# Encoder trunk kernel: four tiles for turned probabilities in the neighbourhood attention, weight splits and a GpSimd multiplication at other places

## The reference, cut to what matters

```
layer 0: x = x + concat(dilated_attention, latent_attention) @ w_out
         x = x + swiglu(rms_norm(x, ln_ffn_e))
layer 1: q, k, v = split(rms_norm(x, ln_mix_o) @ na_w_qkv)        # 16 heads of 64
         sc  = q @ k.T * 64**-0.5 + mask + rpb                    # 256 x 256 a head
         x   = x + (softmax(sc) @ v for every head) @ na_w_out
         logits = rms_norm(x, ln_ffn_o) @ moe_router              # 8 experts, 2 per token
         x   = x + sum over e: gates[:, e] * swiglu_e(rms_norm(x, ln_ffn_o))
out = rms_norm(x, ln_final)
```

## Time and profile before

| what | value |
|---|---|
| median of 3 runs | 1460.08 us (1459.95 to 1460.48) |
| the profiled execution | 1466.72 us, of which the span of the profile is 1464.8 us |
| PE busy | 1430.1 us, 98% |
| DVE, ACT, POOL busy | 1132.6, 969.0, 122.0 us |
| weights read | 426.98 MB from HBM |
| attention heads of layer 1 on PE | about 390 to 452 us from the start of the span |
| output projection | 456.5 to 478.7 us |
| router, to the first expert matmul | 478.4 to 498.4 us |
| experts | 498.4 us to the end |

### The profile page before, as it was taken

The page is one execution under the profiler, slowest core; times in us unless marked ns, Lnnn a source line. Parts: engine busy times, 40 slices in busy tenths (PEclk is TensorE's granted clock), DMA queues, the critical chain, the costliest instruction groups (busy, mean ns, idle before and its releaser), DMA issues.

```text
span 1464.8 us, 20962 instructions
## 1 busy us (share of the span) xinstructions
PE 1430.1 (98%) x7705; PEld 1228.1 (84%) x7705; DVE 1132.6 (77%) x892; ACT 969.0 (66%) x885; POOL 122.0 (8%) x101
## 2 busy tenths in 40 slices
PE   8989999999989999999999999999999999999996
PEld 7878999999988788888888888888888888888885
DVE  4484555556663798988988888888898898888886
ACT  6384543436463577777777777777777777777774
POOL 4141000000000310020001001002002000000100
PEclk8999999999999999999999999999999999999999
DMA  9413755555513599999999999999999999999992
GB/s 337 151 58 102 210 197 173 197 175 173 173 58 111 180 378 378 367 356 394 394 361 394 386 344 393 396 367 376 393 372 364 394 386 354 394 380 363 392 395 109
DMA packets 205562, 434.91 MB, mean 297 GB/s; under 512 B 8160, under 2 KB 53344, under 8 KB 205520
## 3 DMA queue, kind: packets, MB, share of 16 engines
q1 hardware_dynamic: 198176, 418.01, 78.4%
q0 software_dynamic: 3904, 14.42, 3.2%
q10 hardware_dynamic: 3440, 1.91, 0.7%
HBM read 426.98 MB, written 7.34 MB: 297 GB/s over the span
## 4 chain that ended last, share of the span: by engine, by line
PE 92%; DVE 4%; ACT 2%; issue 1%; DMA 0%; DVEq 0%; ACTq 0%
PE banks L1428 29%; PE banks L1430 29%; PE banks L1429 29%; PE banks L1841 2%; PE banks L1650 1%; DVE w_lo L880 1%; PE banks L1638 1%; ACT arena L619 0%; PE banks L1805 0%; DVE arena L1077 0%; DVE small L1083 0%; PE banks L1576 0%; ACT w_hi L469 0%; PE banks L1443 0%; DVE arena L1065 0%
## 5 line engine op out<-in xcount | busy, mean ns | idle before, releaser
L880 DVE TENSOR_TENSOR w_lo<-raw,w_hi 128x2048 fp32r<-128x2048 f32 (+1 forms) x396 | 902.6, 2291 | 223.4 <-ACT w_hi L469 222.0
L469 ACT CAST w_hi<-raw 128x2048 fp32r<-128x2048 f32 (+1 forms) x396 | 756.3, 1910 | 227.2 <-PE banks L1430 219.8
L1428 PE MATMUL banks<-w_hi,t_hi 128*128 128x512 f32 (+2 forms) x1088 | 417.9, 384 | 3.7 <-DVE w_lo L880 1.6
L1430 PE MATMUL banks<-w_lo,t_hi 128*128 128x512 f32 (+2 forms) x1088 | 412.0, 379 | 0.0
L1429 PE MATMUL banks<-w_hi,t_lo 128*128 128x512 f32 (+2 forms) x1088 | 410.9, 378 | 0.0
L1428 PEld LDWEIGHTS banks<-w_hi,t_hi 128*128 128x128 f32 x1088 | 206.2, 190 | 40.9 <-DVE w_lo L880 1.8
L1430 PEld LDWEIGHTS banks<-w_lo,t_hi 128*128 128x128 f32 x1088 | 206.1, 189 | 38.8
L1429 PEld LDWEIGHTS banks<-w_hi,t_lo 128*128 128x128 f32 x1088 | 206.4, 190 | 36.2 <-issue 0.2
L1428 PE MATMUL banks<-w_hi,h_hi 128*128 128x512 f32 x536 | 209.5, 391 | 0.7 <-DVE w_lo L880 0.7
L1430 PE MATMUL banks<-w_lo,h_hi 128*128 128x512 f32 x536 | 208.9, 390 | 0.0
L1429 PE MATMUL banks<-w_hi,h_lo 128*128 128x512 f32 x536 | 208.8, 390 | 0.0
(11 more groups left out here) (269 smaller groups left out, 944.6 us busy)
## 6 DMA issues: line engine op xcount, KB each, us to landing
raw<-in_moe_w_gate SPq DMA_DIRECT2D x112, 1024.0 KB, 7.5
raw<-in_moe_w_up SPq DMA_DIRECT2D x112, 1024.0 KB, 7.8
raw<-in_moe_w_down SPq DMA_DIRECT2D x112, 1024.0 KB, 7.7
raw<-in_na_w_qkv SPq DMA_DIRECT2D x12, 1024.0 KB, 5.2
raw<-in_ffn_w_gate SPq DMA_DIRECT2D x11, 1024.0 KB, 5.5
raw<-in_ffn_w_up SPq DMA_DIRECT2D x11, 1024.0 KB, 5.3
raw<-in_ffn_w_down SPq DMA_DIRECT2D x11, 1024.0 KB, 5.0
raw<-in_w_in_e SPq DMA_DIRECT2D x6, 1024.0 KB, 18.5
```

What stands on the lines that cost most here:

```text
L469: act.copy(w_hi[:, u.part, 0:n], raw[:, u.raw, 0:n]).then_inc(hi_done, 1)
L880: dve.tensor_tensor(w_lo[:, u.part, 0:n], raw[:, u.raw, 0:n], w_hi[:, u.part, 0:n].bitcast(F32), ALU.subtract).then_inc(lo_done, 1)
L1428: pe.matmul(out, a_hi, b_hi, start=start, stop=False)
L1430: return pe.matmul(out, a_hi, b_lo, start=False, stop=stop)
```

## The change

Four things are changed, all in layer 1.

1. Turned probabilities of heads 16 to 31 go through four buffers in turn: the two of `prob_t` and columns 512 to 1023 of the two tiles of `xn`. `prob_out(n)` waits for the values of head n-4 in place of n-2. In the steady loop `prob_out(n - 4)` stands ahead of `softmax(n)`; at the start `softmax(19)` stands ahead of `prob_out(16)`.
2. The three `hi` of the output projection move to the early part of ACT's queue, around `qkv_out(10)` and `qkv_out(11)`, and the three `lo` of DVE to after `row_max` 19, 21 and 22. PE runs `value_unit(2)` ahead of `turn_probs(16)` and `na_scores(4)` ahead of `turn_probs(17)`.
3. The first `keep_busy` has five dummy matmuls in place of eight.
4. GpSimd's two multiplications move to after the transfers of `xres` to `sum_d`.

```diff
+        turned = [prob_t[:, i, :] for i in range(2)]
+        turned_c = turned + [xn[:, t, HALF:D] for t in range(T)]
...
             def prob_out(n):
                 act.wait_ge(pt_mm, n + 1)
-                if n >= 2:
+                if n >= 16:
+                    act.wait_ge(pv_mm, max(n - 3, 16))
+                elif n >= 2:
                     act.wait_ge(pv_mm, n - 1)
-                act.copy(prob_t[:, n % 2, :], banks[:, T_BANK[n % 2], :]).then_inc(pt_out, 1)
+                act.copy(turned_c[n % 4] if n >= 16 else turned[n % 2], banks[:, T_BANK[n % 2], :]).then_inc(pt_out, 1)
...
             softmax(18, "neighbourhood", 2)
+            softmax(19, "neighbourhood", 3)
+            hi(Unit(U_OUT1))
+            qkv_out(10)
+            hi(Unit(U_OUT1 + 1))
             prob_out(16)
-            softmax(19, "neighbourhood", 3)
-            qkv_out(10)
+            softmax(20, "neighbourhood", 4)
             prob_out(17)
-            softmax(20, "neighbourhood", 4)
             softmax(21, "neighbourhood", 5)
-            hi(Unit(U_OUT1))
             qkv_out(11)
+            hi(Unit(U_OUT1 + 2))
             for n in range(22, 16 + CH + 4):
+                prob_out(n - 4)
                 if n < 16 + CH:
                     softmax(n, "neighbourhood", n - 16)
-                prob_out(n - 4)
-                if n in (23, 27):
-                    hi(Unit(U_OUT1 + n // 4 - 4))
...
                 row_max(n, "neighbourhood", n - 16)
-                if n in (21, 25, 29):
-                    lo(Unit(U_OUT1 + n // 4 - 5))
+                if n in (19, 21, 22):
+                    lo(Unit(U_OUT1 + (19, 21, 22).index(n)))
...
             na_scores(3)
+            value_unit(2)
             turn_probs(16)
-            value_unit(2)
+            na_scores(4)
             turn_probs(17)
-            na_scores(4)
             na_scores(5)
...
-            keep_busy(7, 8)
+            keep_busy(7, 5)
             pe.wait_ge(route_v, 1)
...
-            pool.wait_ge(x_tile, X_TILES[4])
-            pool.wait_ge(gain_in[3], 16)
-            for t in range(T):
-                pool.tensor_tensor(xn[:, t, :], xres[:, t, :], gain_rows[1], ALU.mult).then_inc(xg_ready, 1)
...
                 if not sweep:
-                    pool.wait_ge(xg_ready, T)
+                    pool.wait_ge(gain_in[3], 16)
                     for t in range(T):
+                        pool.tensor_tensor(xn[:, t, :], xres[:, t, :], gain_rows[1], ALU.mult).then_inc(xg_ready, 1)
+                    for t in range(T):
+                        pool.wait_ge(xg_ready, t + 1)
                         pool.dma_start(rows_d[t * P:(t + 1) * P, :], xn[:, t, :]).then_inc(rows_out, 16)
```

More of the change, by code:

```diff
@@ L1649, in values @@
                     for k in range(2):
-                        last = pe.matmul(banks[:, 4 + t, c:c + HD],
-                                         prob_t[:, n % 2, (2 * k + t) * P:(2 * k + t + 1) * P], v(k),
+                        p_t = turned_c[n % 4] if n >= 16 else turned[n % 2]
+                        last = pe.matmul(banks[:, 4 + t, c:c + HD], p_t[:, (2 * k + t) * P:(2 * k + t + 1) * P], v(k),
                                          start=(k == 0), stop=(k == 1))
```

## The result

| | before | after |
|---|---|---|
| median of 13 runs each, same chip | 1461.59 us (1459.95 to 1472.41) | 1455.15 us (1452.26 to 1458.11) |
| ratio | | 0.9939, 95% interval 0.9924 to 0.9955 |
| the profiled execution | 1466.72 us, span 1464.8 | 1454.66 us, span 1452.6 |

By the ratio the kernel is 8.9 us faster (1460.08 x 0.0061), between 6.6 and 11.1; the forecast was 10.8. The means of the 13 runs differ by 8.8 us, the two medians of the table only by 6.4. Two things are to be seen at once. The runs of one kernel spread over 6 us and more, so the profiled difference of 12.2 us between the spans is not the effect. And the medians moved with the set of runs (before stands at 1461.6 here, at 1460.1 in its first three), so the absolute 1455.15 lies above the range of 1447.0 to 1453.5, while the ratio, put to 1460.08, gives 1451.2, inside it.

The account below looks back on a forecast made before the run. It took PE, busy 98% of the span, to bound the kernel. Heads 7.2, transposes 0.3 and router 3.3 made 10.8 us, from 1460.1 to 1449.3 us; 8 in 10 for 1447.0 to 1453.5, own gain range 7.5 to 12.9.

Parts of the forecast that it names:

- Heads, 7.2 us: Heads 16 to 31: last values end at 444.6 instead of 451.8 us, 7.2 us earlier; bounds 5.5 and 7.5.
- Copy 18: ACT's copy of head 18's turned probabilities: runs 417.1 to 417.6 us, with 1.1 us to spare.
- the walk: Step-by-step timing of PE, ACT and DVE through the heads in the new order, ending at 444.6 us.
- The split into 6.0 of waits and 1.2 of clock: Of the heads' 7.2 us, 6.0 are waits and 1.2 the clock staying up without PE's 2.02 us wait.
- Four tiles: Heads: with two tiles the copy would wait for values n-2 and hold up the softmax behind it; no size given.
- The transposes, 0.3 us: The 16 transposes behind the heads: 0 to 1.2 us better, by where the lower clock falls; 0.3 taken.
- Router, 3.3 us: Router: DVE's chain and PE's small products start 3.3 us earlier; bounds 2.0 and 4.2 by the clock.
- One of the signs: Prediction wrong if PE's granted clock is 0.5 in stretches other than the few between heads, projection and router.
- `lo` at GpSimd's new place: Beside GpSimd's moved multiplications, one `lo` of DVE waits some 0.8 us, which PE does not see.
- The blocked DVE: Rival: DVE's L1275 waits for GpSimd's products at their new place, 1.5 to 2.9 us lost, 1451.5 us; 10%.
- ACT as the late one: Rival: in the heads ACT's copy 18 misses 418.8, half of the 6 us of waits remain, 1453.5 us; 10%.
- The clock falling in the heads: Rival, slower: heads 16 to 31 at 1.2 GHz, 3.7 us a head, 23 us more, 1473 us; 3%.

Follow-up runs that it names:

- e1: The kernel before with only the heads changed (four tiles, copy ahead, early splits); ratio to before 0.9955, 6.6 us faster.
- e3: The kernel after with the first dummies set back from five to eight; ratio to before 0.9930.
- e5: The kernel after with the old two tiles and the old wait for values n-2; heads 54.27 us in the profile, no ratio.
- e8: The kernel after with GpSimd's multiplications back at the old place, five first dummies kept; router stage 27.43 us in the profile, no ratio.
- e12: As e11, with four more dummies ahead of the transposes before the output projection; ratio to before 0.9923.
- e6: The kernel after with the copy behind the softmax again in the steady loop; heads 65.08 us in the profile, no ratio.
- e7: The kernel after with the three high and three low splits at their old places; heads 60.33 us in the profile, no ratio.
- e2: The kernel before with only the router changed (multiplications behind the transfers, five first dummies); ratio to before 0.9985, 2.2 us faster.
- e11: As e10, with six dummies ahead of each of the first two projection units of layer 0; ratio to before 0.9918.
- e4: The kernel after with eight first dummies and one dummy ahead of each of the eight k steps of the router logits; ratio to before 0.9915.
- e10: The kernel after with eight first dummies and one dummy ahead of every second k step of the router logits; ratio to before 0.9938.

## Why the prediction was right, and where not

- *Heads, 7.2 us.* Right in size and in each step: 7.15 in the profile, 54.21 to 54.27 in every kernel that has both order and splits (e1, e3 to e5, e8 to e12), and 6.6 us (4.2 to 9.1) in the timed runs of e1. Copy 18, the wait of `values(24)` and the last values came within 0.2 us of the walk. The split into 6.0 of waits and 1.2 of clock fits the old trace, with 5.4 us of waits for the copy and 3.4 us at half the clock; e6 and e7 show that the clock can also cost more with a wait of 2 us.
- *Four tiles.* I named them as something that would otherwise hold up the softmax. The wait exists, its cost does not: 0.05 us (e5). What carries is the place of the copy (e6) and of the splits (e7), each alone enough to bring PE's wait of 2 us back.
- *The transposes, 0.3 us.* Nothing: 3.62 against 3.53, still at the lower clock. Where the clock was up, in e2, e11 and e12, they took 1.97 and the stage from the last values on took 25.7 in place of 26.7, so the upper bound of 1.2 was about right.
- *Router, 3.3 us.* This is the step that failed. Its DVE half is exact: copies and subtractions at 0.69 and 1.22, the chain at the square sums, the product 3.3 us earlier, L1275's like undisturbed. But I put the lower clock at what it was before, shifted, with 2.0 as the worst. It lasted 17.1 us in both profiles of after, took the products, the dummies, the gather and the first expert matmuls, and left -1.1 us there; in the six profiles with this router the term is between -1.4 and +1.3, outside its bounds of 2.0 and 4.2 each time. One of the signs that I had named for a wrong prediction, a granted clock of 0.5 in further stretches, is met. Over the timed executions e2 gives 2.2 us (0 to 4.4), which agrees with the term and with much less. `lo` at GpSimd's new place, put at 0.8 us that PE does not see, does not wait in after; in e4 it waits 2.7 us and PE 0.6.
- *The sum.* 6.6 (e1) and 2.2 (e2) make 8.8; measured 8.9 (6.6 to 11.1), against 10.8. The heads carry it. That the total lies inside the forecast's own range of 7.5 to 12.9 has some luck in it: the profiled pair of before and after gives 6.0 for the stages touched, and the absolute 1455.15 lies above 1453.5; only the ratio, put to the first three runs of before, falls inside.
- *The rivals.* The blocked DVE did not come. ACT as the late one did not come either, copy 18 having its slack. The clock falling in the heads did not come in after, but in e6 and e7 with waits left in, and e6 is slower than before in the heads. I had put a head at 1.2 GHz at 3.7 us; in e6 one takes 4.2 (from 440.30: 0.88 of transposes, 1.74 of scores, 1.59 of values), so that rival was priced too low. I had asked whether denser small work lets the clock fall; in before, e6 and e7 a wait of 2 us goes with the fall, which came inside it in the first two and 1.7 us behind it in e7. That the wait is the cause is not shown.

## What to carry to other kernels

Where two engines hand work to and fro in written-out order, put the short instruction that the bound engine waits for ahead of the long one that waits for something else; here this and moving six splits gave all of the heads' gain, and two more tiles gave none. Keep large GpSimd products away from DVE's copies and from its operations with two SBUF inputs on the path, and put them beside operations that read PSUM; look also at what stands next in DVE's queue once the stage gets faster. A gain of a few us in a stage of small matmuls is worth only what the tensor clock leaves of it: look at the granted clock of the stage in several executions before you believe a stage time.

## What the runs showed of the hardware that was not expected

The granted clock fell while PE was busy without a gap: 5.00 of 5.00 us between 465 and 470, with transposes and the logits' products, then 0.53. The Trainium skill, "TensorE: Matmul & The Clock Gate", in its part on the clock gate, has the gate follow how busy PE has been; by PE's busy time in the profile this trace does not agree, since the level fell right behind 5.00 us of full busy time. Once down it stayed for 10.2 to 17.1 us in eight of the eleven profiles with GpSimd's products at the new place, though dummies lay inside; in e12 it was down for 3.4 us, and in e4 and e11 not at all. These three have dummies among the logits, and so has e10, which was down for 10.2.

An execution's level at the start (1.2 GHz for 10.2 us from 18 to 20 us on, or not) goes with a shift of the whole by some 5 us, more than half of what this change brings: the first scores stand at 389.0 to 390.6 with it (seven profiles) and at 384.2 to 385.7 without it (seven). What decides it stays open.
